# Conv block of a two-layer streaming encoder: combination, norm and split ordered by frame half

## The reference, cut to what matters

```
layer 0:  h = h + mixers(rmsnorm(h));      h = h + moe(rmsnorm(h))     # 32 experts, 2 per frame
layer 1:  z = rmsnorm(h) @ w_in_c          # 1024 -> 3 x 1024: bg, cg, hh
          u = cg * hh
          conv_t = sum_j u[t-2+j] * conv_w[j]       (j = 0, 1, 2)
          h = h + (bg * conv) @ w_out_c;   h = h + moe(rmsnorm(h))
```

## Time and profile before

| | |
|---|---|
| median of 3 runs | 1318.99 us (1318.32 to 1322.79) |
| the profiled execution | 1317.1 us, its span 1315.0 us |
| PE busy | 1068.6 us, 81% of the span |
| DVE, ACT, POOL busy | 470.3, 284.7, 214.1 us |
| last matmul of layer 0's experts ends | 758.3 us |
| first matmul of the conv loop | 802.95 us |
| last matmul of the conv loop | 950.5 us |
| last instruction of the conv block's input split | 802.5 us |

### The profile page before, as it was taken

The page is one execution under the profiler, slowest core; times in us unless marked ns, Lnnn a source line. Parts: engine busy times, 40 slices in busy tenths (PEclk is TensorE's granted clock), DMA queues, the critical chain, the costliest instruction groups (busy, mean ns, idle before and its releaser), DMA issues.

```text
span 1315.0 us, 17971 instructions
## 1 busy us (share of the span) xinstructions
PE 1068.6 (81%) x7539; PEld 800.8 (61%) x7539; DVE 470.3 (36%) x961; ACT 284.7 (22%) x549; POOL 214.1 (16%) x154
## 2 busy tenths in 40 slices
PE   5999997775997974997778817999998499787881
PEld 5899997653565753554444417999976365444440
DVE  5233761765544153111111056456435311111114
ACT  5243321200441120211111133222112111111110
POOL 3334332012203000221111100000000022111110
PEclk9999998885797985999888857999998699999996
DMA  6321324003000259999999881333254999999985
GB/s 199 88 94 65 97 79 98 1 14 127 18 1 6 96 227 351 386 415 416 417 416 415 316 237 52 97 96 91 69 81 162 353 382 417 415 417 416 416 341 213
DMA packets 110686, 282.56 MB, mean 215 GB/s; under 512 B 22890, under 2 KB 61846, under 8 KB 94196
## 3 DMA queue, kind: packets, MB, share of 16 engines
q1 hardware_dynamic: 100884, 263.66, 53.8%
q0 software_dynamic: 9728, 17.85, 3.6%
HBM read 270.57 MB, written 27.02 MB: 226 GB/s over the span
## 4 chain that ended last, share of the span: by engine, by line
PE 58%; DMA 16%; DVE 11%; SPq 9%; ACT 2%; issue 2%; POOL 2%; DVEq 0%; POOLq 0%; ACTq 0%
DMA w<-in_w_dram 11%; PE bank L978 11%; PE bank L899 10%; PE bank L843 9%; PE bank L637 8%; SPq L375 6%; PE bank L910 4%; PE bank L636 3%; SPq L378 2%; PE bank L802 2%; DMA wab<-in_w_in_ab_dram 2%; PE bank L773 2%; DVE XN L1226 1%; PE bank L612 1%; DMA yab<-y_rows 1%
## 5 line engine op out<-in xcount | busy, mean ns | idle before, releaser
L899 PE MATMUL bank<-w,xgT 128*64 128x256 f32 x2048 | 259.7, 414 | 65.0 <-DMA w<-in_w_dram 64.3
L899 PEld LDWEIGHTS bank<-w,xgT 128*64 128x64 f32 x2048 | 160.0, 150 | 173.1 <-DMA w<-in_w_dram 70.5
L1574 DVE TENSOR_TENSOR hh<-bank,sg 128x128 f32<-128x128 f32 x64 | 18.7, 292 | 405.5 <-ACT sg L1160 405.5
L565 POOL DMA_INDIRECT y_rows<-ys,yidx x64 | 63.6, 994 | 379.7 <-ACT ys L1168 378.4
L910 PE MATMUL bank<-w,hT 128*64 128x512 f32 x512 | 116.9, 598 | 0.0
L978 PE MATMUL bank<-xc_hi,wc_hi 128*128 128x272 f32 x384 | 111.8, 291 | 1.4 <-DVE xc_lo L1239 1.4
L978 PE MATMUL bank<-xc_hi,wc_lo 128*128 128x272 f32 x384 | 112.2, 292 | 0.0
L978 PE MATMUL bank<-xc_lo,wc_hi 128*128 128x272 f32 x384 | 111.5, 290 | 0.0
L561 POOL DMA_INDIRECT xr<-x_rows,gidx x32 | 33.5, 1046 | 398.1 <-DVE yidx L1557 373.5
L637 PE MATMUL bank<-wab_hi,xc_hi 128*128 128x256 f32 (+1 forms) x320 | 90.4, 283 | 0.7 <-POOL wab_lo L532 0.7
L637 PE MATMUL bank<-wab_hi,xp_lo 128*128 128x256 f32 (+1 forms) x320 | 90.2, 283 | 0.0
(11 more groups left out here) (283 smaller groups left out, 1856.9 us busy)
## 6 DMA issues: line engine op xcount, KB each, us to landing
w<-in_w_dram SPq DMA_DIRECT2D x192, 1024.0 KB, 22.8
wab<-in_w_in_ab_dram SPq DMA_DIRECT2D x13, 1024.0 KB, 5.0
wc<-in_w_in_c_dram SPq DMA_DIRECT2D x24, 512.0 KB, 6.2
yab<-y_rows SPq DMA_DIRECT2D x16, 512.0 KB, 7.0
wo<-in_w_out_ab_dram SPq DMA_DIRECT2D x2, 2048.0 KB, 10.5
x_rows<-XN SPq DMA_DIRECT2D x8, 512.0 KB, 20.4
woc<-in_w_out_c_dram SPq DMA_DIRECT2D x2, 2048.0 KB, 8.2
H<-in_x_prompt_dram SPq DMA_DIRECT2D x4, 512.0 KB, 8.4
```

The lines of the kernel that those rows point to most:

```text
L565: pool.indirect_dma_start(y_dram[l][:, :], bass.IndirectOffsetOnAxis(ap=index.bitcast(U32), axis=0), ys[i][:, :], None, bounds_check=4 * T ...
L899: last = pe.matmul(bank[hb][64 * f:64 * f + 64, 0:2 * P].rearrange("p (w j) -> p w j", w=2), xgT[i][:, k, 64 * ab:64 * ab + 64], w13[s][:, ...
```

## The change

- `yab` of chunks 2, 3 and 4 moves to other addresses, free at that time.
- SP loads only weight block 0 ahead of the wait for the scatters; block 1 is loaded behind the ten `yab` loads, ahead of the norm gain.
- DVE: combinations 0 and 1, norm 0, combination 2, norm 1, low part 0, norm 2, low parts 1 and 2; then combinations 3 and 4, norm 3, low part 3, norm 4, low part 4. `combine` is the former loop body as a function.
- ACT: the squares and high parts in the same order; the high part of weight block 1 comes behind the last chunk's high part. The high part of `woc` half 0 comes at the end of m = 1, behind that of weight block 3; its low part on DVE at the start of m = 2.
- PE: transposes of chunks 0 to 2, then half 0 of m = 0 begins when chunks 0 to 2 are split; chunk 3 is transposed behind its second product, chunk 4 behind its third; half 1 waits for all chunks. The loop is written out in place of a hardware loop.

```diff
-        yab = [at(f"yab{c}", 132 + 8 * c, [P, 2, D]) for c in range(NC)]
+        yab = [at(f"yab{c}", (132, 140, MISC, MISC + 8, MISC + 16)[c], [P, 2, D]) for c in range(NC)]
@@ SP
-                    for s in range(2):
-                        sp.wait_ge(y_mm, 27 + s)
-                        conv_load(s, s)
+                    sp.wait_ge(y_mm, 27)
+                    conv_load(0, 0)
...
+            conv_load(1, 1)
             sp.dma_start(gffn[:], norm_ffn[1:2, :].partition_broadcast(P)).then_inc(gffn_in, 16)
@@ PE
-            norm_transposes(2)
-            pe.wait_ge(xt_a, NC * 3)
-            pe.wait_ge(xt_d, NC * 3)
-            with pe.Fori(0, KT // 2) as i:
...
+            def frames_ready(c):
+                pe.wait_ge(xt_a, NC * 2 + c)
+                pe.wait_ge(xt_d, NC * 2 + c)
+            for c in range(3):
+                norm_transpose(2, c)
+            for m in range(KT):
+                pe.wait_ge(wc_lo_ok, m + 1)
+                for half in range(2):
+                    if m == 0:
+                        frames_ready(3 if half == 0 else NC)
+                    pe.wait_ge(cg_ok, 2 * m + half + 1)
+                    for a in range(3):
+                        conv_terms(m, half, a)
+                        if m == 0 and half == 0 and a >= 1:
+                            norm_transpose(2, a + 2)
@@ ACT
             conv_hi(0)
+            square(2, 0)
+            square(2, 1)
+            mixer_in_hi(2, [0])
+            square(2, 2)
+            mixer_in_hi(2, [1, 2])
+            for c in (3, 4):
+                square(2, c)
+                mixer_in_hi(2, [c])
             conv_hi(1)
-            squares(2)
-            mixer_in_hi(2)
-            conv_out_hi(0)
             for m in range(KT):
...
                 if m + 2 < KT:
                     conv_hi(m + 2)
+                if m == 1:
+                    conv_out_hi(0)
@@ DVE
-                for c in range(NC):
...
-                    if l == 0 and c > 0:
-                        norm(2, c - 1)
-                if l == 0:
-                    norm(2, NC - 1)
+                    combine(l, 0)
+                    combine(l, 1)
+                    norm(2, 0)
+                    combine(l, 2)
+                    norm(2, 1)
+                    mixer_in_lo(2, xc_lo, [0])
+                    norm(2, 2)
+                    mixer_in_lo(2, xc_lo, [1, 2])
+                    combine(l, 3)
+                    combine(l, 4)
+                    for c in (3, 4):
+                        norm(2, c)
+                        mixer_in_lo(2, xc_lo, [c])
...
-            mixer_in_lo(2, xc_lo)
...
-            conv_out_lo(0)
             for m in range(KT):
+                if m == 2:
+                    conv_out_lo(0)
```

More of the change, by code:

```diff
@@ L964, in _, with conv_terms @@
             mixture(0)
-            norm_transposes(2)
-            pe.wait_ge(xt_a, NC * 3)
-            pe.wait_ge(xt_d, NC * 3)
-            with pe.Fori(0, KT // 2) as i:
[L971 to L981, removed]
+            def conv_terms(m, half, a):
+                s = m % 2
+                for k in range(KT):
+                    for j, (w, x) in enumerate(((wc_hi, xc_hi), (wc_hi, xc_lo), (wc_lo, xc_hi))):
+                        last = pe.matmul(bank[3 * half + a][:, 0:HALF], w[s][:, k, a, :], x[:, k, half * HALF:(half + 1) * HALF],
+                                         start=k == 0 and j == 0, stop=k == KT - 1 and j == 2)
+                if a == 2:
+                    last.then_inc(c_mm, 1)
+            def frames_ready(c):
[13 more added lines that the diff above has]
+                            norm_transpose(2, a + 2)
             def z_c(part, k):
@@ L1616, in mixture, with combine @@
                     conv_lo(0)
-                for c in range(NC):
[L1618 to L1623, removed]
-                    if l == 0 and c > 0:
-                        norm(2, c - 1)
-                if l == 0:
-                    norm(2, NC - 1)
+                    combine(l, 0)
[11 more added lines that the diff above has]
+                        mixer_in_lo(2, xc_lo, [c])
+                else:
+                    for c in range(NC):
+                        combine(l, c)
+            def combine(l, c):
+                n = ROWS[c]
+                dve.wait_ge(rows_in[c], 16 + 32 * (l + 1))
+                h = H[0:n, c, :]
+                for i in range(2):
+                    tie(dve.scalar_tensor_tensor(h, yab[c][0:n, i, :], gate[i][0:n, c:c + 1], h, ALU.mult, ALU.add))
+                dve.nop().then_inc(h_ok, 1)
             def conv_lo(m):
```

## The result

Over 20 runs of each, the changed kernel takes 1325.76 us median (1319.12 to 1328.34), before 1319.13. The ratio is 1.0036, 95% interval 1.0023 to 1.0049: 4.7 us slower, where I had 1.35 us faster and a range that ended at 1322. (The two medians lie 6.6 us apart; the executions of each kernel spread over 9 to 13 us, and I go by the ratio.) The profiled execution took 1322.69 us, its span is 1320.3.

A forecast was written before the change was run, and what follows sets the result against it. PE, busy 81% of the span, was taken as the bound, waiting near the change only between 758 and 803 us. 10.6 gained - 6.75 stall - 2.5 clock = 1.35 us less: 1317.6 us from 1318.99, range 1311.5 to 1322.

The forecast's parts named there:

- Step 1: Ahead of the loop: with block 1's load behind the `yab` loads, the last scatter lands and rows return 3.15 us earlier.
- layer 0 and layer 1 differ in more than the weight load: Rival at layer 0's last scatter: rows don't come earlier, 3.15 us less gain, 1320.8 us; chance 0.10.
- Step 2: Loop start: half 0 begins after three chunks, at 791.9 us, or 788.75 with the earlier rows, against 802.95 before.
- C: Stage from first conv matmul to ACT's `hc` of block 0's half 1; hand-back there was forecast to leave 10.6 us gain.
- the two terms named there: Inside block 0, between its halves: 1.0 us of transposes and 2.9 us of hand-over come off the gain.
- the clock's fall in the hand-over: Rival between block 0's halves: short idles drop PE's clock, another 2.5 us lost, 1320.1 us; chance 0.10.
- step 4: Between blocks 1 and 2: the moved `woc` split stalls PE 6.75 us ahead of block 3, plus 2.5 us slow clock.
- D: Stage from ACT's `hc` of block 0's half 1 to first projection matmul; forecast 6.75 us stall and 2.5 slow clock.
- Everything behind the loop (...) shifts as a whole: Projection and layer 1's experts, behind the conv loop: claimed to move together with the loop's end, with no term of their own.

The follow-up runs named there:

- e5: e1 with weight block 1's load put back ahead of the wait for the scatters; ratio 0.9992 to the kernel before, where e1 has 0.9988.
- e7: The changed kernel with PE's blocks 2 to 7 in a hardware loop of three pairs, blocks 0 and 1 written out; ratio 1.0045 to the kernel before.
- e1: The changed kernel with the split of the first half of `woc` moved to the loop's end; ratio 0.9988 to the kernel before.
- e2: The kernel before with only the split of `woc`'s first half moved between blocks 1 and 2; ratio 1.0102, 13.4 us slower.
- e8: The changed kernel with only squares and norms of chunks 3 and 4 put ahead of their high and low parts; ratio 1.0026 to the kernel before.
- e11: e4 with one wait added: PE starts block 3 only when DVE has gated half 1 of block 2; ratio 1.0006 to the kernel before.
- e4: e1 with squares and norms of chunks 3 and 4 both ahead of their high and low parts; ratio 0.9947 to the kernel before.
- e3: The kernel before with only PE's conv loop written out in place of a hardware loop; ratio 1.0024, 3.2 us slower.

## Why the prediction was wrong

**Start of the loop: right in size, its parts off.** Forecast 14.2 us from scatter to first matmul, measured 6.71 + 36.50 - 5.18 - 24.34 = 13.7. Step 1's 3.15 was mis-sized: it measured 1.5 here. I had put the whole difference between the two layers' last scatters down to block 1's load. That load did go (no packet of it lies beside the scatter in after), and the last scatter but one then landed in 2.35 us where before had 5.07. The last one didn't: it took 4.03, and an instruction packet moved beside it, which layer 1 of before doesn't have. Over all profiles, of the scatters with no weight load beside them, 24 without an instruction packet landed in 2.35 to 2.61 us and 19 with one in 3.21 to 4.39. That the packet is what delays them is not shown by an experiment of its own. My rival "layer 0 and layer 1 differ in more than the weight load" was half right. Step 2 gave 1.1 us more than forecast, 0.4 of it by faster first rows.

**Block 0: short by 1.5 us, a step that failed.** C grew by 5.2, forecast 3.6 (the two terms named there, 1.0 and 2.9, make 3.9; the 3.6 comes from 24.5 less 20.9). The order of events was as written, within half a us. What failed is that I gave the clock's fall in the hand-over a chance of 0.10 and no term; it fell in the changed kernel, in e5 and in e7, 14 or 15 slow matmuls each, which is 1.5 us.

**The stall of step 4: right.** Forecast 6.75 us of idle and 2.5 of slow matmuls, measured 6.9 and 21 slow matmuls (0.227 us apart in place of 0.126); D grew by 9.35 against 9.25. e1 and e2 show that the `woc` split makes it, by taking it out and by putting it in alone.

**Behind the loop: the other step that failed.** "Everything behind the loop (...) shifts as a whole" is wrong. In all five profiles in which PE stood 4.0 us or more inside the loop (after, e2, e7, e8, e11) layer 1's router logits, 150 us and more later, ran slow, 5.78 to 6.94 us; in all nine others they took 4.09. From layer 1's first weight load to its first gather the changed kernel takes 64.75 us where before takes 63.14, e2, e8 and e11 66.5.

The granted clock shows what lies between. It falls behind the projection in every profile, where PE has little to do (in before it works 0.86 of the 3.9 us ahead of the fall), and the logits follow about 13 us after the projection's end. In windows (columns as in the earlier trace rows) of e4, then after, then e11:

```profile
1002.60:1009.30 6.70, 4.39 (x19) 3.58 (x20) 3.98 (x7) 1.88 (x4) 0.00 (x0) 0.50 1.02 426
1009.40:1016.30 6.90, 5.85 (x47) 3.84 (x45) 1.53 (x5) 0.97 (x3) 0.00 (x0) 1.00 1.01 420
```

```profile
1018.90:1022.15 3.25, 2.23 (x20) 1.53 (x20) 1.57 (x4) 0.88 (x2) 0.00 (x0) 1.00 1.04 439
1022.30:1025.55 3.25, 3.25 (x18) 2.03 (x15) 0.00 (x0) 0.00 (x0) 0.00 (x0) 0.50 1.01 408
```

```profile
1009.45:1022.95 13.50, 11.66 (x54) 8.46 (x56) 3.70 (x7) 1.59 (x4) 0.00 (x0) 0.50 1.02 422
```

In e4 the clock is back at its upper level for the logits; in after it comes back and falls once more, in their midst; in e11 it stays low into them. Which of the three happens goes with how soon the fall comes after the projection's last matmul: 3.17 and 3.26 us in e7 and after, 3.35 to 5.33 in the nine with fast logits, 5.53 to 5.72 in e11, e2 and e8. After and e4 are only 0.09 us apart in this. So in these profiles the logits' time goes with how the work lies against the clock's changes. A stall, at which the clock falls and rises anew, goes with a shift of that: from the clock's last rise in the loop to the projection's end it is 143.5 to 144.7 us in the five, 189 to 203 in the nine. e11 against e4 puts the slow logits beside an added wait and nothing else, but with one profile of each; whether another execution of e4 or of before has them too is not shown.

Last in the chain, layer 1's last scatter lands 1.1 us later than in before (3.48 to 2.40), with the instruction packet beside it that e3 has as well. I gave the written-out program no term.

So the forecast of -1.35 becomes, by the profiles, +0.5 (start), +1.5 (block 0), +0.1 (stall), +1.6 (logits and gather), +1.1 (layer 1's experts and end): 3.4 us slower, which is the difference of the two spans less the 1.8 ahead of the last scatter. The measured interval is 3.0 to 6.5. It is partly luck that they meet: the last scatter is issued anywhere from 759.7 to 766.1 us over the 14 profiles, and 2.0 us apart in the two of before. What is left between 3.4 and 4.7 stays open. The rank of the rivals was wrong in the same way: I had the clock's fall as a rival that ends at 1320.1, and priced each idle time by the matmuls right behind it alone.

## What to carry to other kernels

Work that moves out of a free place must find another: here 8 us of ACT and DVE lay beside the first products and ended 5 us before DVE was next wanted; between blocks 1 and 2 they had 1.4 us of slack, and at the end a whole free block, where e1 and e4 put them without a stall. Before an edit that starts PE earlier, list what PE's late start was hiding, and give each piece its slack at the new place. A stall inside an otherwise dense run of matmuls can cost more than its length: the pairs that differ by one (e11 and e4, e2 and before, e8 and e4, after and e1) have 4.0, 6.4, 6.8 and 6.9 us of idle and 7.8, 13.4, 10.4 and 6.3 us of time, each to about 3 us. The early start with the stall lost 4.7 us; without it and with the norms ahead (e4) it gained 7.0 (4.5 to 9.4). And two profiles of one kernel can differ by where the clock happens to fall, so a stage of a single profile is not yet a price.

## What was not expected of the hardware

The granted clock at a late stretch went with an idle time long before it: 31 logit matmuls at 4.09 us in nine profiles and at 5.78 to 6.94 in the five with a stall in the loop, with dense matmuls for over 90 us between. Two profiles in which the clock fell behind the projection only 0.09 us apart had 4.09 and 5.78. An idle time's length alone didn't decide whether the clock fell: between the halves of block 0 the starts of the products lay 2.75 to 2.76 us apart in after, e5, e7 and e1; the clock fell in the first three, where full speed had come 5.8 us or more after the loop's start, and not in e1, where it came after 3. An indirect scatter took 5.4 to 5.6 us while a weight block landed beside most of it, and 3.2 to 4.4 with no weight load at all but one instruction packet beside it, where 2.35 to 2.61 is its time with neither.
